# Layer norms by token halves, with the mean subtracted on GpSimd, in a two-layer decoder trunk

## The reference

```python
for l in range(2):
    h = layer_norm(a * h + 0.5 * swiglu(h, ffn1_w_gate[l], ffn1_w_up[l], ffn1_w_down[l]), ln1_g[l], ln1_b[l])
    z = h @ w_in[l]                       # u_pool | q | k | v | r | g_lowrank
    y = concat([pool_mixer(u_pool, ...), gla_mixer(q, k, v, r, g_lr, ...)]) @ w_out[l]
    h = layer_norm(a * h + y, ln2_g[l], ln2_b[l])
    h = layer_norm(a * h + 0.5 * swiglu(h, ffn2_w_gate[l], ...), ln3_g[l], ln3_b[l])
return h[:, 16:]

def layer_norm(x, g, b):
    mu = mean(x); var = mean(square(x - mu))
    return (x - mu) * rsqrt(var + 1e-5) * g + b
```

## Time and profile before

| | |
|---|---|
| Time of the runs | 1822.68 us median of 3 (1822.0 to 1826.67) |
| Profiled execution | 1826.83 us, span 1825.1 us |
| PE busy | 1796.3 us (98%) |
| DVE, ACT, POOL busy | 1426.1, 1163.6, 327.4 us |
| Mean granted TensorE clock | 0.983 |

### The profile page before, as it was taken

One profiled execution on the slowest core, in us unless ns is written; L12 is line 12 of the kernel. 1 busy time (PEld: TensorE's weight loads), 2 busy tenths in 40 slices (PEclk: granted clock), 3 DMA queues, 4 the chain that ended last, 5 costly groups with the idle time before them and its releaser, 6 DMA issues.

```text
span 1825.1 us, 37497 instructions
## 1 busy us (share of the span) xinstructions
PE 1796.3 (98%) x14400; PEld 1745.5 (96%) x14400; DVE 1426.1 (78%) x2558; ACT 1163.6 (64%) x2030; POOL 327.4 (18%) x366
## 2 busy tenths in 40 slices
PE   8999999999999999999999999999999999999997
PEld 8999999999999999999999999999998879999996
DVE  6888888668457888888688888886684579888886
ACT  6667676574346667676576676765743466777764
POOL 2111111210010111112311111112100111212113
PEclk9999999899998999999999999998999989999998
DMA  7675757556554676766656757665565646767661
GB/s 205 141 183 130 181 130 166 120 136 136 118 121 101 159 176 136 175 136 157 148 127 136 180 130 183 129 162 127 135 132 116 138 96 163 178 138 185 132 165 70
DMA packets 114081, 263.54 MB, mean 144 GB/s; under 512 B 10736, under 2 KB 37872, under 8 KB 113904
## 3 DMA queue, kind: packets, MB, share of 16 engines
q1 hardware_dynamic: 68112, 167.86, 31.8%
q0 software_dynamic: 45504, 92.29, 30.1%
q10 hardware_dynamic: 288, 0.98, 0.2%
HBM read 259.00 MB, written 2.10 MB: 143 GB/s over the span
## 4 chain that ended last, share of the span: by engine, by line
PE 91%; DVE 5%; ACT 2%; issue 1%; DMA 1%; ACTq 0%; DVEq 0%; SPq 0%
PE PS L631 20%; PE PS L632 20%; PE PS L633 20%; PE PS L610 3%; PE PS L611 3%; PE PS L612 3%; PE PS L567 3%; PE PS L565 3%; PE PS L566 3%; PE PS L575 2%; PE PS L601 2%; PE PS L576 2%; PE PS L925 1%; PE PS L760 1%; DMA raw<-in_stream 1%
## 5 line engine op out<-in xcount | busy, mean ns | idle before, releaser
L505 POOL DMA_DIRECT2D w_lo<-in_stream x316 | 269.3, 852 | 1412.4 <-ACT w_lo L1136 1377.4
L1132 ACT ACTIVATE s_hi<-s_sum 128x512 fp32r<-128x512 f32 (+1 forms) x496 | 291.2, 588 | 160.2 <-PE PS L633 145.0
L1583 DVE TENSOR_TENSOR s_lo<-s_sum,s_hi 128x512 fp32r<-128x512 f32 (+1 forms) x496 | 294.0, 634 | 2.9 <-ACT s_hi L1132 2.6
L631 PE MATMUL PS<-v_hi,s_hi 128*128 128x264 f32 (+1 forms) x912 | 259.3, 284 | 4.2 <-ACT u_copy L1215 4.0
L633 PE MATMUL PS<-v_hi,s_lo 128*128 128x264 f32 (+1 forms) x912 | 257.9, 283 | 0.0
L632 PE MATMUL PS<-v_lo,s_hi 128*128 128x264 f32 (+1 forms) x912 | 257.8, 283 | 0.0
L633 PE MATMUL PS<-x_hi,w_lo 128*128 128x264 f32 (+1 forms) x656 | 185.6, 283 | 0.0
L631 PE MATMUL PS<-x_hi,w_hi 128*128 128x264 f32 (+1 forms) x656 | 185.5, 283 | 0.0
L632 PE MATMUL PS<-x_lo,w_hi 128*128 128x264 f32 (+1 forms) x656 | 185.5, 283 | 0.0
L631 PEld LDWEIGHTS PS<-v_hi,s_hi 128*128 128x128 f32 x912 | 171.7, 188 | 5.5 <-ACT u_copy L1215 4.8
L632 PEld LDWEIGHTS PS<-v_lo,s_hi 128*128 128x128 f32 x912 | 172.1, 189 | 0.0
(11 more groups left out here) (274 smaller groups left out, 5721.9 us busy)
## 6 DMA issues: line engine op xcount, KB each, us to landing
raw<-in_stream SPq DMA_DIRECT2D x164, 512.0 KB, 4.3
w_lo<-in_stream POOLq DMA_DIRECT2D x160, 256.0 KB, 4.6
spare<-in_stream SPq DMA_DIRECT2D x72, 512.0 KB, 6.9
w_lo<-in_stream POOLq DMA_DIRECT2D x60, 512.0 KB, 7.8
raw<-in_stream SPq DMA_DIRECT2D x48, 384.0 KB, 4.2
spare<-in_stream SPq DMA_DIRECT2D x48, 384.0 KB, 5.4
w_lo<-in_stream POOLq DMA_DIRECT2D x96, 192.0 KB, 4.8
X<-in_x_t SPq DMA_DIRECT2D x8, 264.0 KB, 6.8
```

The lines of the kernel that those rows point to most:

```text
L505: pool.dma_start(w_lo[:, slot, to], stream[n // RAWS, n % RAWS, :, part], accum_op=ALU.add).then_inc(lo_added[slot], 16)
L631: nc.tensor.matmul(o, hi[:, w], r_hi, start=start and k == 0, stop=False, skip_group_check=True)
L1132: nc.scalar.activation(s_hi[:, j - 1, w], s_sum[:, j - 1, w], ACT.Copy).then_inc(S["s_hi_done"], 1)
L1583: V.tensor_tensor(s_lo[:, j - 1, w], s_sum[:, j - 1, w], s_hi[:, j - 1, w].bitcast(F32), ALU.subtract).then_inc(S["s_lo_done"], 1)
```

## The change

1. *Ends.* The order of output tiles at a stage's end becomes a list `ENDS` of twelve: tiles 0 to 3 whole, tiles 4 to 7 for the first token half, then tiles 4 to 7 for the second. The mixer's end uses four PSUM pairs instead of two. Sums and squares follow the twelve ends.
2. *Statistics by halves.* Columns, spreads, variance, standard deviation and diagonals are done once for each half. Those of the first half stand on PE between and inside ends 8, 9 and 11 (`amid_end`, `after_end`); those of the second stand after the products of units 0, 1 and 3 of the next stage.
3. *Units.* The next stage's first products go by 14 units: tiles 0 to 5 for the first half, tiles 0 to 5 for the second, tiles 6 and 7 whole (`UNITS`, `unit_products`). The low passes of a unit come behind the high passes of the next. In an FFN the third piece's `w_lo` pass is taken out and done behind all units.
4. *Centers.* POOL subtracts the mean from `X` in place, in 14 units, at three places of its queue of weight pieces. `xhat` is gone. DVE multiplies by gain and spread deviation in one step, in place. ACT adds the bias into `x_hi`; DVE makes `x_lo` as (X + bias) - `x_hi` in one step; the bias is added to `X` later, for tiles 0 to 3 by POOL and for 4 to 7 by ACT (by POOL before the mixer).
5. *The rest.* `v_sums` and `take_pool_part` wait for the full `X`. The parameter load of layer 1 moves behind the first silu of its FFN. With 512 tokens the stage ends, the first products, the fourth piece's product and the two plain ones use halves of 256. The last norm is in 16 half tiles, with a store for each.

The diff, cut to its core:

```diff
+SPLIT_TILES = 6
+ENDS = tuple([(mo, None) for mo in range(4)] + [(mo, p) for p in range(2) for mo in range(4, KC)])
+def units_of(split):
+    return [(k, p) for p in range(2) for k in range(split)] + [(k, None) for k in range(split, KC)]
...
+            def center(norm, unit, span):
+                k, p = unit
+                tok = unit_tokens(span, p)
+                pool.wait_ge(S["mean_copied"], 2 * norm + (1 if p == 0 else 2))
+                pool.wait_ge(S["sq_done"], norm * len(ENDS) + (8 if p == 0 else len(ENDS)))
+                nc.gpsimd.tensor_tensor(X[:, k, tok], X[:, k, tok], mean[:, tok],
+                                        ALU.subtract).then_inc(S["pool_centered"], 1)
+            def full(norm, k, span):
+                tok = slice(span[0], T)
+                pool.wait_ge(S["x_lo_done"], norm * len(UNITS) + last_unit(k) + 1)
+                nc.gpsimd.tensor_scalar(X[:, k, tok], X[:, k, tok], norm_bias(norm % LN_PER, k), None,
+                                        ALU.add).then_inc(S["x_full_done"], 1)
             for n in range(SLOTS, DEPTH * LAYER_PIECES):
+                for norm in range(DEPTH * LN_PER - 1):
+                    at, span = n - next_stage(norm), span_of(norm)
+                    if at == 2:
+                        for unit in UNITS[0:SPLIT_TILES]:
+                            center(norm, unit, span)
+                    elif at == 3:
+                        for unit in UNITS[SPLIT_TILES:SPLIT_TILES + 2]:
+                            center(norm, unit, span)
+                    elif at == 4:
+                        for unit in UNITS[SPLIT_TILES + 2:]:
+                            center(norm, unit, span)
+                        pool.wait_ge(S["par_loaded"], norm // LN_PER * 16 + 16)
+                        for k in range(POOL_TILES):
+                            full(norm, k, span)
...
+                for u in range(len(UNITS)):
+                    high_passes(u)
+                    if u == 0:
+                        sum_columns(norm, span, 1)
+                    elif u == 1:
+                        square_columns(norm, span, 1)
+                    elif u == 3:
+                        spread_rstd(norm, span, 1)
+                    if u > 0:
+                        low_passes(u - 1)
...
+                for i in range(4, 9):
+                    square(i)
+                copy_mean(0)
+                root(0)
+                square(9)
+                if not final:
+                    piece_high(nxt + 2)
+                square(10)
+                shifted(0)
+                square(11)
+                shifted(1)
+                shifted(2)
+                copy_mean(1)
+                if not final:
+                    piece_negative(nxt + 2)
+                root(1)
+                for u in range(3, SPLIT_TILES):
+                    shifted(u)
+                if not final:
+                    piece_high(nxt + 3)
+                    piece_negative(nxt + 3)
+                for u in range(SPLIT_TILES, len(units)):
+                    shifted(u)
...
+                    V.scalar_tensor_tensor(out=x, in0=x, scalar=par[:, C_LN + 16 * r + k:C_LN + 16 * r + k + 1], in1=rstd,
+                                           op0=ALU.mult, op1=ALU.mult).then_inc(S["xhat_done"], 1)
+                    V.scalar_tensor_tensor(out=x_lo[:, k, tok], in0=X[:, k, tok], scalar=norm_bias(r, k),
+                                           in1=x_hi[:, k, tok].bitcast(F32), op0=ALU.add, op1=ALU.subtract)\
+                        .then_inc(S["x_lo_done"], 1)
...
+                resid(8)
+                add_sum(8)
+                mean_column(0)
+                add_square(8)
+                variance(0)
+                resid(9)
+                diagonals(0)
+                add_sum(9)
+                add_square(9)
+                resid(10)
+                add_sum(10)
+                add_square(10)
+                scale(0)
+                resid(11)
+                add_sum(11)
+                scale(1)
+                add_square(11)
+                scale(2)
+                mean_column(1)
+                scale(3)
+                variance(1)
...
+                lo(0)
+                diagonals(1)
+                lo(1)
+                scale(4)
+                lo(2)
+                scale(5)
+                lo(3)
+                lo(4)
```

## The result

The change makes the kernel slower: 1862.03 us (1860.59 to 1863.59, four runs) against 1823.64 us (1822.0 to 1826.67, four runs), a ratio of 1.0208 with a 95% interval of 1.0196 to 1.022. The forecast was 1820.5 us and its range ended at 1832.

A forecast was written before the change was run, and what follows sets the result against it. PE was taken to bound the kernel, busy 1796.3 of 1825.1 us. Terms: -6.4 + 4.0 - 1.5 + 1.0 + 0.7 = -2.2 us, so 1824.6 from the profiled 1826.83, or 1820.5 on the median; range 1803 to 1832.

The forecast's parts named there:

- GpSimd centers in place: At the norms, POOL's mean subtracts take turns with DVE's sums, diagonals and low parts; PE's waits rise from 2.4 to 4.5 us.
- The clock: PE's clock at the five norm boundaries: one or two falls taken, 2.7 us per boundary, 4.0 us in all.
- the slower rival: Clock falls at every boundary and the bias step takes 1.3 us or more: +11.3 us, 1834.0; chance 0.20.
- The bias step: POOL's bias add on 528 columns, behind the centers in its queue: 0.9 us assumed, bounds 0.55 and 1.3.
- The walk of the halves: Queues walked in their new order at a norm boundary, the last four tiles as eight halves: 2.4 us of waits before collisions.
- The 6.4 us: Gain at the five norm boundaries together, with 5.0 us of waits each and the clock held at 1.00.
- W: PE's waits at a norm boundary beyond its products and statistics: 5.0 us used, 2.4 without collisions.
- the end: The kernel's last norm in 16 half tiles, each with a store: 14.5 us against 13.8, +0.7; without collisions -1.4.
- the 512-token layout: 312 matmuls of 512 columns become 624 of 256, 0.004 us more per pair: +1 us.
- the FFN's start: PE's 4.0 us wait at the first Strassen-like product shrinks 0.5 us per FFN behind a norm: 1.5 us gained.
- Free overlap: At the norms, DVE's slack swallows collisions with POOL and the clock holds: 21.3 us faster, 1801.4; chance 0.22.
- The FFN takes it back: X full later, so the first Strassen-like product waits 1 to 2 us more: 1824 to 1827; chance 0.08.

The follow-up runs named there:

- the separate kernel: A kernel computing nothing of the reference: GpSimd chains beside four VectorE operations, with or without a DMA issue ahead; first operation 4.72 us behind an issue.
- two versions of this one: The changed kernel with a one-column memset and a wait on GpSimd ahead of the second and third center groups, 1832.96 us, or the third alone, 1842.95 us.
- with the chains cut: The changed kernel with a one-column memset and a wait for it on GpSimd ahead of the second and third groups of centers: 1832.96 us.
- second profile: The kernel before the change, unchanged, profiled again: 1823.47 us, span 1821.7.
- with VectorE's centers: The changed kernel with VectorE, not GpSimd, subtracting the mean ahead of each scale in the five norms between stages: 1831.59 us.
- the best version: The changed kernel with VectorE centering units 0 to 5, GpSimd the others behind a drain, low passes three units behind, scales first: 1828.47 us.
- one pair of versions: Low passes three units behind, without and with scales first: mixed VectorE/GpSimd centers 1834.95 and 1828.47 us; the other pair, GpSimd's centers, 1833.09 and 1832.42.

## Why the prediction was wrong

*The step that failed* is the collision model under "GpSimd centers in place": "DVE's sums, diagonals and low parts take turns with POOL", and "later ones hold low parts of units 6, 9 and 10: 0.2 + 0.3 + 0.5 us more". It was read from the earlier trace rows, where each subtract waits for its own data, and no row of before has a subtract right behind a DMA issue. The change puts its second and third groups exactly there, in the queue of weight pieces. One operation per group is held for the rest of the chain. Cutting the chains gives back 29.1 of the 41.5 us between the forecast and the measured time (and of the 38.4 us between the two kernels). That the chain behind the issue does it is shown, in the separate kernel and in two versions of this one. How, is not shown. Subtracts behind an issue last 1.05 us at a distance of 0.71, so that one begins before the last has ended, and may leave no opening, where the others last 0.74; but adds behind an issue overlap as well (1.9 us long, 1.6 apart) and let VectorE in between. Nor does a run tell whether the memset or the wait for it is what breaks the chain.

*The clock*: one or two falls of five were taken, and all five fell. That was the slower rival's condition, but not as a cause of its own: with the chains cut, two fell (the 0.86 and 0.81 above), as had been taken. The price of the others is part of the 29 us.

*The bias step* was taken at 0.9 us with bounds of 0.55 and 1.3; it is 1.6 to 2.5 in after, and 1.60 in the separate kernel where VectorE has nothing beside it. The estimate by the Trainium skill's *GPSIMD Engine Reference* § Elementwise — side-by-side cycle accounting, 0.6 us, was further off. A version without it on GpSimd is no faster and waits no less for low parts (30.3 us), so "with 1.3 us the last low parts wait more" is not borne out, at least beside the held chains.

*The walk of the halves* held where its model of turns did. First product: 1.9 us behind the last half's end forecast, 2.1 of idle measured; low pass of unit 0: 0.9 forecast, 0.7 with the chains cut. Centers take 0.71 and 1.25 us from start to start (0.68 and 1.28).

*But the total was still too good.* With the chains cut and two falls of the clock, the forecast's own terms should give 1820.5 us, and 1833 came. Four things make up most of these 12.5 us.

The first is where the gain was counted from. The 6.4 us were read off the first profile, of the slowest execution of before, and carried to the median by "the same difference". The second profile shows that 3.2 us of that execution's length stood in the five windows themselves (133.8 against 130.6), in the waits and slow matmuls that the change replaces.

The second is the boundaries. With the 1.9 us of statistics that now stand ahead of each, the three at full clock take 27.0, 25.5 and 26.5 us where 26.4, 24.5 and 25.6 were forecast; with the two falls, the five are some 3 us over. In the first two the products need 17.4 and 15.5 and the second half's statistics 1.5, so W is 6.2 and 6.55, not 5.0; part of that was covered, because the forecast charged 4.0 us for statistics, which take 3.4 with the slow matmuls behind them. The waits by name are 4.0 us in each of the two; the rest is in small gaps, most of them at a change of unit, which a walk with one duration per matmul doesn't have. And statistics between the halves cost more than their own time. PE in the first norm of after:

```profile
347.58 0.56 PE L906 MATMUL PS<-ones_mean,sum_x 128*88 128x1 f32 x6
347.99 0.69 PE L916 MATMUL PS<-sum_x,ones_mean 128*128 128x264 f32 x2
348.33 0.48 PE L640 MATMUL PS<-h_hi,w_hi 128*128 128x264 f32 x1
348.64 0.28 PE L641 MATMUL PS<-h_lo,w_hi 128*128 128x264 f32 x1
```

The first dense matmul behind them takes 0.31 us to its follower instead of 0.12. At all three places the statistics take 1.4 us and these first matmuls 0.5 more: 1.9 us per norm, 1.75 in the two with 512 tokens, 11.1 in six. The stretches between the windows grew by 10.9 us in after and by 13.9 with the chains cut. With the chains cut, the five windows plus their share of this, 9.4 us, come to 134.3 (124.9 + 9.4), against 130.6 in the second profile of before.

The third is the end. With the chains cut the last window is 0.5 us longer than in the second profile of before, with 1.75 us of statistics ahead of it, so 2.3 longer; 0.7 was forecast. In after it is 1.0 shorter, so 0.8 longer, though nothing in the last norm differs between the two: it varies by 1.5 us from one profile to the other.

The fourth is the rest of the stretches. With the chains cut they hold 2.8 us beyond the statistics, where the forecast has 1.0 for the 512-token layout and 1.5 back at the FFN's start. PE's waits at the first Strassen-like product are 3.8 us, against 3.7 in the second profile of before: nothing came back. In after they are 1.8, with VectorE's centers 1.6, in the best version 4.1; why, no run shows. The layout's own cost can't be told either: the two stretches with 512 tokens grew by no more than the others (2.3 and 1.1 us, against 1.4 to 3.5).

*The rivals.* Free overlap (1801) is refuted by the turns. "The FFN takes it back" didn't occur. The slower rival had the right side, and both its conditions came, five falls and a bias step over 1.3 us; but it put 13.5 us on the falls and 3.0 on the bias step, knew nothing of the held operations, and came to 1834, 28 us short. That with the chains cut the kernel took 1833 us is not this rival's mechanism: two falls, and W for other reasons.

What stays open: the last 4 to 5 us between the best version and before. VectorE's order was worth 6 us in one pair of versions and under 1 in the other, and no run separates VectorE's total from ScalarE's queue. Nor did a run put the first half's statistics elsewhere, though their 11.1 us are most of the 14.1 by which that version's stretches between the windows grew.

## What to carry to other kernels

Before putting elementwise work on GpSimd into a queue that also issues DMAs, look at what stands right ahead of it: a chain of two-input subtracts directly behind an issue shut VectorE's operations with two SBUF inputs out to its end here, and one memset with a wait for it restored turns. When a trace gives the price of a contention, check that the new place has the same neighbour ahead, not just the same pair of operations. And when work is cut finer to fill a wait, count each change of matmul kind on TensorE and each extra pair of operations on VectorE first: here, with the chains cut, the windows, without the first half's statistics, took 5.7 us less and the stretches between them 13.9 more. And count a gain from more than one profile of the kernel before: half of this one was in the execution that had been profiled.

## What the hardware showed

- A chain of GpSimd subtracts directly behind a DMA issue held one VectorE operation with two SBUF inputs up to 6.20 us, against turns of 0.97 without the issue. The hold begins before the first subtract's recorded start: diagonals of 0.42 us, begun 0.49 us ahead of it inside the issue, took 2.49 us.
- One-input adds on GpSimd leave VectorE nearly alone (2.06 us for four operations, 1.70 with no chain at all), except behind a DMA issue (5.80 us, one operation at a time).
- A one-input GpSimd add of 528 columns with its scalar in SBUF takes 1.60 us alone, more than the two-input subtract's 1.25 from start to start.
- The first dense matmul behind one-column matmuls and spreads takes 0.20 to 0.32 us to its follower, against 0.12.
